# Context rows as 32 tokens at 4 slots, summed in four column groups, with U and V fetched as one row

## What is computed

```
s = jnp.einsum('thpd,hpnd->thpn', qf, sub_keys)
...
act = jax.nn.gelu(jnp.einsum('td,thkd->thk', xb, u_tab[ib]), approximate=False)
return jnp.einsum('thk,thkd->td', gb * act, v_tab[ib])
```

## Time and profile before

| what | value |
|---|---|
| median of three runs | 3763.48 us (3762.64 to 3769.86) |
| the profiled execution's own time | 3768.37 us |
| its span in the trace | 3766.6 us |
| mean granted PE clock | 0.946 |
| busy over the span: PE, DVE, ACT, POOL | 87%, 76%, 25%, 37% |
| data moved over the span | 336 GB/s |

### The profile page before, as it was taken

How to read it: one execution, slowest core, us unless ns; L and a number is a source line. 1 busy time by engine, 2 the same in 40 slices (tenths; PEclk the granted TensorE clock), 3 DMA queues, 4 the chain that set the end, 5 groups by cost and what they waited for, 6 DMA issues and landing times.

```text
span 3766.6 us, 32345 instructions
## 1 busy us (share of the span) xinstructions
PE 3291.4 (87%) x9441; PEld 1672.5 (44%) x9441; DVE 2851.2 (76%) x6490; ACT 928.8 (25%) x2415; POOL 1375.1 (37%) x1205
## 2 busy tenths in 40 slices
PE   7678989987897988577777789999999999999998
PEld 4355434433543444234433444444454444444444
DVE  2637797659767878888898589888787888777776
ACT  1322221355422111146634501011011101110111
POOL 1000554546654445333233222333333333333331
PEclk9889999999998999788998899999999999999999
DMA  9243876768888899999999999999999999999996
GB/s 349 76 176 132 291 247 224 256 221 297 298 307 309 297 346 333 393 360 360 337 396 383 370 365 396 386 404 403 409 411 411 416 391 404 416 409 409 407 409 271
DMA packets 305103, 1269.03 MB, mean 337 GB/s; under 512 B 29456, under 2 KB 79888, under 8 KB 218656
## 3 DMA queue, kind: packets, MB, share of 16 engines
q0 software_dynamic: 169200, 959.16, 65.8%
q1 hardware_dynamic: 134000, 302.17, 21.5%
q10 hardware_dynamic: 1728, 5.64, 0.4%
HBM read 1217.28 MB, written 49.58 MB: 336 GB/s over the span
## 4 chain that ended last, share of the span: by engine, by line
PE 26%; issue 23%; DVE 22%; DMA 19%; POOL 7%; ACT 3%; SPq 0%; DVEq 0%; POOLq 0%; ACTq 0%
DMA arena<-in_uv,idx 7%; DMA ring_e<-in_uv,idx 6%; PE bank L902 5%; PE bank L930 3%; PE wide L845 3%; DMA ring_e<-in_v_rows,idx 3%; PE bank L1064 3%; DVE arena L1873 3%; POOL arena L791 3%; POOL ring_e L791 2%; DVE ring_e L1873 2%; DVE ring_e L1813 2%; PE wide L1114 2%; DVE arena L1904 2%; PE bank L1094 2%
## 5 line engine op out<-in xcount | busy, mean ns | idle before, releaser
L791 POOL DMA_INDIRECT arena<-in_uv,idx x384 | 454.8, 1184 | 845.8 <-PE bank L1126 506.1
L1169 PE MATMUL bank<-arena 128*128 128x384 f32 x2048 | 695.7, 494 | 55.8 <-ACT arena L1569 34.6
L1873 DVE CUSTOM_DVE_ANT_0 arena<-arena,h2e 128x1024 f32<-128x1024 f32 x384 | 460.8, 1220 | 150.3 <-DMA arena<-in_uv,idx 149.3
L1169 PEld LDWEIGHTS bank<-arena 128*128 128x128 f32 x2048 | 392.2, 193 | 370.2 <-issue 136.4
L791 POOL DMA_INDIRECT ring_e<-in_uv,idx x256 | 296.2, 1157 | 618.4 <-PE bank L1126 350.8
L750 POOL DMA_INDIRECT ring_e<-in_u_rows,idx x256 | 330.7, 1292 | 486.7 <-DVE dots_e L1813 332.5
L1182 PE MATMUL wide<-arena 128*128 128x512 f32 x1024 | 462.2, 594 | 5.6 <-DVE arena L1943 5.5
L1512 ACT ACTIVATE small<-small 128x4 f32<-128x4 f32 x160 | 32.7, 205 | 1416.8 <-DVE small L1873 1416.8
L1873 DVE CUSTOM_DVE_ANT_0 ring_e<-ring_e,h2e 128x1024 f32<-128x1024 f32 x256 | 306.8, 1219 | 85.1 <-DMA ring_e<-in_uv,idx 84.9
L1813 DVE CUSTOM_DVE_ANT_0 ring_e<-ring_e,h2e 128x1024 f32<-128x1024 f32 x256 | 303.1, 1219 | 50.6 <-DMA ring_e<-in_u_rows,idx 48.6
L845 PE MATMUL wide<-ring_e,diag_e 128*128 128x512 f32 x520 | 258.7, 638 | 83.4 <-ACT diag_e L1236 55.4
(11 more groups left out here) (265 smaller groups left out, 4424.4 us busy)
## 6 DMA issues: line engine op xcount, KB each, us to landing
arena<-in_ut SPq DMA_DIRECT2D x128, 512.0 KB, 7.9
arena<-in_uv SPq DMA_DIRECT2D x128, 512.0 KB, 8.3
arena<-in_w_q SPq DMA_DIRECT2D x48, 512.0 KB, 6.8
spread_d<-arena SPq DMA_DIRECT2D x12, 2048.0 KB, 25.4
arena<-spread_d SPq DMA_DIRECT2D x96, 256.0 KB, 10.7
ring_e<-in_w_mod POOLq DMA_DIRECT2D x16, 1024.0 KB, 8.1
arena<-in_w_cols SPq DMA_DIRECT2D x24, 512.0 KB, 5.5
arena<-in_x SPq DMA_DIRECT2D x20, 512.0 KB, 4.6
```

The costliest lines, as they stand in the source:

```text
L791: pool.indirect_dma_start(out=ring[r], out_offset=None, in_=a["uv"], in_offset=bass.IndirectOffsetOnAxis(ap=idx[kept(t)][:, k:k + 1], axis ...
L1169: ins = pe.matmul(s_bank[:, 0:NC], lhsT=utb[i % URING][:, k * P:(k + 1) * P], rhs=H2T[1][:, k, P:P + NC], start=(k == 0), stop=(k == KD - 1))
L1873: dve.tensor_tensor_reduce(out=ring[r][:, 0:D], in0=ring[r][:, 0:D], in1=h2b[kept(t)], scale=1.0, scalar=0.0, op0=ALU.mult, op1=ALU.add, a ...
```

## The change

1. **One gather a slot.** U and V come as one 8 KB row of the joint table (`uv`), by one indirect DMA (`gather_row`), which waits for the sum of slot k − 4 (`used_e`). The ring stays at four slots.
2. **Another shape of a slot.** A slot is now 32 tokens at 4 of their experts: partition 32·s + t holds token t's s-th one. `h2e` therefore holds 32 tokens in four copies, in two buffers that change every 32 slots; POOL loads them between the gathers (`load_tokens`, 4 DMAs). `idx` and `gate` of tiles 0 and 1 are put into that order by 16 small DVE operations each in place of one, and `idx_ready` is signalled between the two.
3. **All sums on PE, in column groups.** The weight matrix of a slot is 128x32 (`diag_e[...][:, 0:32]`, made from `sel32`, four 32x32 identities above each other), which adds the four experts of each token. Four matmuls 128x32 by 256 go to the four groups of 32 output partitions, one for each quarter of the row. DVE's sums are gone, and so is `vector_sums`.
4. **The finish of tiles 0 and 1.** Their sums now lie as 32·j partitions by 256·g columns, so the gate, the residual, the squares (`squares_e`, folded over the four quarters by `fold_squares` on PE in beats 1 and 4), the norm and the store run in that layout, with loads and stores in four pieces. SP's load of tile 2's input moves from the start of the last block of score rounds to its round 8.

The core of the diff:

```diff
+        sel32 = gain_reg[:, 3 * P:3 * P + Q]
...
-        hooks, by_vector, at_hook = {}, [], 0
-        for phase, n, vector in (("conv", 16, (False, True)), ("qk", 9, (False,)), ("vg", 16, (False, True)),
-                                 ("ln", 8, (False,)), ("gates", 8, (False,)), ("states", 14, (False,)),
-                                 ("attn", 10, (False,)), ("out", 16, (True,)), ("qf0", 16, (True,)), ("qf1", 16, (True,))):
+        hooks, at_hook = {}, 0
+        for phase, n in (("conv", 16), ("qk", 9), ("vg", 16), ("ln", 8), ("gates", 8), ("states", 14), ("attn", 10),
+                         ("out", 16), ("qf0", 16), ("qf1", 16)):
...
-        def vector_sums(k):
-
-            return k % SLOTS >= EC and by_vector[k // EC]
-
-        def used_e(k):
-
-            return S["used_v" if vector_sums(k) else "used_e"].at(k)
...
-                        sp.wait_ge(*S["dot_e"].at(SLOTS - 1))
-                        load_h2(2)
...
+                        if b == 2 and hp == HP // 2:
+                            sp.wait_ge(*S["dot_e"].at(2 * SLOTS - Q - 1))
+                            load_h2(2)
...
+            def load_tokens(n):
+
+                for i in range(4):
+                    pool.dma_start(h2e[n % 2][i * Q:(i + 1) * Q, :], h2_d[n * Q:(n + 1) * Q, :]
+                                   ).then_inc(*S[f"h2e_in{n % 2}"].mark(n, 16))
+
             pool.wait_ge(*S["h2_out0"].at(0))
-            pool.wait_ge(*S["h2_out1"].at(1))
-            for t in range(2):
-                pool.dma_start(h2e[t], h2_d[t * P:(t + 1) * P, :]).then_inc(*S["h2e_in"].mark(0, 16))
+            for n in range(2):
+                load_tokens(n)
             pool.wait_ge(S["idx_ready"].sem, 1)
 
-            def gather_u(k):
+            def gather_row(k):
 
                 if k == SLOTS:
                     pool.wait_ge(S["idx_ready"].sem, 2)
                 if k >= ERING:
-                    pool.wait_ge(*S["dot_e"].at(k - ERING))
+                    pool.wait_ge(*S["used_e"].at(k - ERING))
                 pool.indirect_dma_start(
-                    out=ring_e[k % ERING][:, 0:D], out_offset=None, in_=a["u_rows"],
+                    out=ring_e[k % ERING], out_offset=None, in_=a["uv"],
                     in_offset=bass.IndirectOffsetOnAxis(ap=idx[k // SLOTS][:, k % SLOTS:k % SLOTS + 1], axis=0)
-                ).then_inc(*landed_u[k % ERING].mark(k, 16))
-
-            def gather_v(k):
-
-                if k >= ERING:
-                    pool.wait_ge(*used_e(k - ERING))
-                pool.indirect_dma_start(
-                    out=ring_e[k % ERING][:, D:2 * D], out_offset=None, in_=a["v_rows"],
-                    in_offset=bass.IndirectOffsetOnAxis(ap=idx[k // SLOTS][:, k % SLOTS:k % SLOTS + 1], axis=0)
-                ).then_inc(*landed_v[k % ERING].mark(k, 16))
-
-            for k in range(2 * SLOTS + V_BEHIND):
-                if k < 2 * SLOTS:
-                    gather_u(k)
-                if k >= V_BEHIND:
-                    gather_v(k - V_BEHIND)
+                ).then_inc(*landed_e[k % ERING].mark(k, 16))
+
+            for k in range(2 * SLOTS):
+                gather_row(k)
+                if k % Q == ERING - 1 and k > Q and k < (2 * SLOTS) - Q:
+                    load_tokens(k // Q + 1)
                 if k == 3:
+                    pool.wait_ge(*S["h2_out1"].at(1))
...
-                    if vector_sums(k):
-                        continue
-                    if k % SLOTS and vector_sums(k - 1):
-                        pe.wait_ge(*used_e(k - 1))
                     pe.wait_ge(*S["diag_e"].at(k))
-                    pe.wait_ge(*landed_v[k % ERING].at(k))
-                    for h in range(2):
-                        ins = pe.matmul(wide[k // SLOTS][:, h * 512:(h + 1) * 512], lhsT=diag_e[k % ERING],
-                                        rhs=ring_e[k % ERING][:, D + h * 512:D + (h + 1) * 512],
-                                        start=(k % SLOTS == 0), stop=(k % SLOTS == SLOTS - 1), skip_group_check=True)
+                    pe.wait_ge(*landed_e[k % ERING].at(k))
+                    c0 = k // Q % 4 * (D // 4)
+                    for j in range(4):
+                        ins = pe.matmul(wide[k // SLOTS][j * Q:(j + 1) * Q, c0:c0 + D // 4], lhsT=diag_e[k % ERING][:, 0:Q],
+                                        rhs=ring_e[k % ERING][:, D + j * (D // 4):D + (j + 1) * (D // 4)],
+                                        start=(k % Q == 0), stop=(k % Q == Q - 1), skip_group_check=True)
                     ins.then_inc(*S["used_e"].mark(k))
...
+            def fold_squares(t):
+
+                pe.wait_ge(*S["y_sum"].at(t))
+                bk = bank(("fold", t))
+                for j in range(4):
+                    ins = pe.matmul(bk[j * Q:(j + 1) * Q, 0:4], lhsT=sel32, rhs=fss[:, 0:4], start=True, stop=True,
+                                    skip_group_check=True)
+                full(ins, ("fold", t))
...
+                if g0 == 0:
+                    act.wait_ge(S["pick"].sem, chain_at(t_ + 1))
...
-                for j in range(0 if vector_sums(k0) else EC):
+                for j in range(EC):
                     act.wait_ge(*S["weight_e"].at(k0 + j))
                     if k0 + j >= ERING:
-                        act.wait_ge(*used_e(k0 + j - ERING))
-                    act.activation(diag_e[r0 + j], ident[:], ACT.Copy, scale=wts_e[:, r0 + j:r0 + j + 1]
+                        act.wait_ge(*S["used_e"].at(k0 + j - ERING))
+                    act.activation(diag_e[r0 + j][:, 0:Q], sel32, ACT.Copy, scale=wts_e[:, r0 + j:r0 + j + 1]
                                    ).then_inc(*S["diag_e"].mark(k0 + j))
...
+            def squares_e(t):
+
+                act.wait_ge(*S["y_pre"].at(t))
+                for g in range(4):
+                    c = slice(g * (D // 4), (g + 1) * (D // 4))
+                    ins = act.activation(ybuf[:, c], x1b[t][:, c], ACT.Square, accum_out=fss[:, g:g + 1])
+                ins.then_inc(*S["y_sum"].mark(t))
...
+                        quarters = [(slice(g * Q, (g + 1) * Q), slice(s * Q, (s + 1) * Q)) for g in range(4) for s in range(4)]
+                        if tile < STREAMS[0][1]:
+                            for g, s in quarters:
+                                done(dve.scalar_tensor_tensor(out=idx[p][s, g], in0=pi[0][g, s], scalar=float(NKEYS),
+                                                              in1=pi[1][g, s], op0=ALU.mult, op1=ALU.add))
+                            after()
+                            dve.sem_inc(S["idx_ready"].sem)
...
+                            hq = PH // 4
+                            for i, (g, s) in enumerate(quarters):
+                                h = slice(i % 4 * hq, (i % 4 + 1) * hq)
+                                done(dve.tensor_tensor(gate[p][s, g].rearrange("p (h k) -> p h k", k=TOPK), g3[g, h, :],
+                                                       gsum[g, h].unsqueeze(2).to_broadcast([Q, hq, TOPK]), ALU.mult))
...
-                    early_sums(c - 1)
                     early_dots(c)
-
-            def early_sums(c):
-
-                for k in range(EC * c, EC * c + EC):
-                    if c < 0 or not vector_sums(k):
-                        continue
-                    t_, r_ = k // SLOTS, k % ERING
-                    dve.wait_ge(*used_e(k - 1))
-                    dve.wait_ge(*S["weight_e"].at(k))
-                    dve.wait_ge(*landed_v[r_].at(k))
-                    dve.scalar_tensor_tensor(out=wide[t_][:], in0=ring_e[r_][:, D:2 * D], scalar=wts_e[:, r_:r_ + 1],
-                                             in1=wide[t_][:], op0=ALU.mult, op1=ALU.add).then_inc(*S["used_v"].mark(k))
...
-                    dve.wait_ge(*S["h2e_in"].at(0))
                 for k in range(EC * c, EC * c + EC):
-                    r_ = k % ERING
-                    dve.wait_ge(*landed_u[r_].at(k))
+                    r_, n = k % ERING, k // Q
+                    if k % Q == 0:
+                        dve.wait_ge(*S[f"h2e_in{n % 2}"].at(n))
+                    dve.wait_ge(*landed_e[r_].at(k))
                     if k >= ERING:
                         dve.wait_ge(*S["gelu_e"].at((k - ERING) // EC))
-                    dve.tensor_tensor_reduce(out=ring_e[r_][:, 0:D], in0=ring_e[r_][:, 0:D], in1=h2e[k // SLOTS], scale=1.0,
+                    dve.tensor_tensor_reduce(out=ring_e[r_][:, 0:D], in0=ring_e[r_][:, 0:D], in1=h2e[n % 2], scale=1.0,
...
+                    dve.wait_ge(*S["mod_rows"].at(2))
+                    dve.tensor_reduce(sel32, ident[:].rearrange("p (s t) -> p t s", t=Q), AX.X, ALU.add
+                                      ).then_inc(*S["sel32"].mark(0))
```

More of the change, by code:

```diff
@@ L311, in build @@
         w_in = [signal(f"w_in{i}") for i in range(WSLOTS)]
-        landed_u = [signal(f"landed_u{i}") for i in range(ERING)]
-        landed_v = [signal(f"landed_v{i}") for i in range(ERING)]
+        landed_e = [signal(f"landed_e{i}") for i in range(ERING)]
```

(20 more changed lines are left out.)

93 lines of the change are left out of this document (65 added, 28 removed).

## The result

The changed kernel takes 4014.04 us (median of 4 runs, 4012.68 to 4017.86) against 3763.66 us (4 runs of the kernel before on the same chip): a ratio of 1.0663 (95% interval 1.0645 to 1.0682), 250 us slower. Its profiled execution has a span of 4015.7 us and a mean granted clock of 0.907, where the one before had 3766.6 and 0.946.

What follows compares the result with a forecast made beforehand. No single engine bounds the kernel: PE paces projections, ln and score rounds, DVE gates and states. Terms 161 + 55 - 43 - 14 + 4 - 2 + 8 + 3 = +172 on 3763.5 give 3935 us, range 3850 to 4030.

Steps and rivals of the forecast that it cites:

- The chain of the score rounds: Score rounds: PE's sums wait for dots behind the copy of scores PE just made, so each round is serial; +161 us.
- PE's idle time in a round: Score rounds, sign in the trace: PE idles some 6 us ahead of the sums, ended by ACT's diagonals; below 2 refutes.
- conv to ln with the start: Projections -43 and ln -14 us from shorter sums on PE; start +3 for tile 0's extra small index operations.
- the ring: Gates and states: a slot is free for the next U row only after its sum; +4 us, between 0 and +37.
- the clock: Score rounds: PE's waits lower the granted clock to 0.81 from 0.97; +55 us, ends 0 and +86.
- attention and all behind the rounds: Attention: smaller diagonals save 0.2 to 0.3 us a hook, -2 us, ends 0 and -24; behind the rounds: 0.
- Rival 4: Ring late everywhere: rows land in 12.3 us, slots freed by the sum; gates and states +37, 3968 us; chance 0.08.
- Out: Output projection: PE gets 17 us of sums, DVE loses 41; +8 us, ends +17 and -24.
- Rival 1: Score rounds: PE doesn't wait, as the diagonals are ready when its scores end; 3710 us; chance 0.06.
- Rival 2: DMA is the limit and 8 KB rows relieve it, 8.6% more rate in the score rounds; 3673 us; chance 0.04.
- Rival 3: Column groups run one after the other, a pair's sums stay at 3.44 us on 89 hooks; 4148 us; chance 0.04.
- Rival 5: It all cancels: waits in the rounds half as long, every gain at its far end; near 3763 us; chance 0.02.

## Why the prediction was right, step by step

**Direction, place and mechanism held.** The loss came out at 250 us where 172 were forecast; 4014 lies within the range, 16 us from its upper end. The chain of the score rounds was put at +161 us at full clock, and the run that keeps PE busy measured +163. PE's idle time in a round was put at some 6 us. It is 5.99 in qf0 (8.45 where a tile is normalised) and 4.03 in qf1, where the chain is shorter, ended by ACT's diagonals each time. The rounds come every 17.3 to 17.6 us in qf0 (19.7 to 20.1 where a tile is normalised) and every 14.7 and 16.0 in turn in qf1 (17 and 15 predicted). Moving the sums by one round took 208 us away, moving the dots by 2 us took 39.

The other 78 us are mostly four terms that missed on the same side: conv to ln with the start 28, the ring 27 (gates and states 13.5, out 13.4), the clock 13.5, and attention and all behind the rounds 6. The range held the time because it left 95 us above the forecast, not because these terms were right.

**The clock was mis-sized by 13 us.** The step took 0.81 on 8.97 us of work, +55; the run measured 68.5. The windows show 0.79 and 0.83, so the mean was right. But PE's work is not spread evenly over it: the sums, which follow the idle time, take 1.94 against 1.07 in all of qf0 but the first round and in every second round of qf1 (1.6 in the others), and the projection behind them takes 8.2 to 9.3 instead of 7.1.

**The ring was priced too low.** The prediction charged gates and states +4 and nothing elsewhere, with a landing of 8 us for two hooks and the clock at its former level outside the rounds. They came out at +17.5, and two gathers bring back 16.6 of it. The single gather also costs 14 us in out and 6 to 8 in conv to ln; attention is 6.5 shorter with it, and the medians differ by 28. Rival 4 named this mechanism and priced it at +37, all in gates and states; the runs put it at half of that there, and at 11 (by the medians) to 16 us (by the traces) elsewhere. A single landing was about right: in gates and states it is 7.6 us in the median, where the half rows of the kernel before took 5.9 and 6.1. But the two gathers of a pair are in flight one behind the other (one pair there was issued at 842.07 and 843.37 and landed at 847.43 and 851.18), and in the median the second lands 9.5 us after the first was issued. And the sums that free the slots take 1.94 instead of 1.05 at a clock of 0.52 in gates. That gives (9.5 + 4.5 + 0.9)/2 = 7.4 a hook, an estimate from these numbers, of the 176.3/22 = 8.0 that were measured; the rest is open. Whether the later release or the longer landing of the 8 KB rows weighs more, no run tells apart, since each changed both.

**Conv to ln gave 26 us of the 57 forecast (54 with the start).** Three things make up most of the gap. The single gather took 8 (446.1 to 438.0). Tile 1's rearranging was left out: the prediction counted tile 0's 15 extra small operations before its first gather, and not that tile 1's 32 run in the midst of the q/k projections, ahead of DVE's convolution step and of the dots that PE waits for. The timeline of DVE and PE in the changed kernel:

```profile
513.24 3.40 DVE L1794 SCALAR_TENSOR_TENSOR idx<-pi 32x32 uint32<-32x32 f32 x16
...
517.35 3.40 DVE L1815 TENSOR_TENSOR gate<-ge,small 32x32 f32<-32x32 f32 x16
520.78 2.98 DVE L2070 TENSOR_SCALAR arena<-arena,cw,cvv 128x1024 f32<-128x1024 f32 x4
...
524.86 1.22 DVE L1849 CUSTOM_DVE_ANT_0 ring_e<-ring_e,h2e 128x1024 f32<-128x1024 f32 x1
...
528.24 1.93 PE L836 MATMUL wide<-ring_e,diag_e 128*32 128x256 f32 x16 [7.01 <-ACT diag_e L1241]
```

The two rows of 16 take 6.8 us, where two single operations took 0.29 each before, and PE waits 7 us for the dots behind them. In the kernel with the new layout for tile 0 only, the sum at the same place waits 0.89:

```profile
517.38 1.07 PE L863 MATMUL wide<-ring_e,diag_e 128*32 128x256 f32 x16 [0.89 <-ACT diag_e L1271]
```

There conv to ln were another 6.8 shorter than with two gathers alone (438.0 to 431.2). And a pair costs 1.19 on the path, not 1.05: hooks of v come every 8.06 us, less 6.87 for the projection. Over the 49 hooks that is 7. What is left of the gap, some 6 us, was not tried; kernels with the same code in these stages differ by 5.

**Out:** +8 was right for the sums alone (152.1 with two gathers, +7.1); the rest of the +21.4 goes with the gather.

**Rivals 1, 2, 3 and 5** are out: PE waits 4 to 6 us a round; the single gather by itself makes the kernel before 30 us slower, with DMA as busy in the rounds as it was; a pair takes 1.07 of PE's time, so the column groups run at once; and nothing cancelled.

## What to carry to other kernels

Before work is moved to another engine, look at what stands directly ahead of it there and at what its inputs wait for: a piece that needs an answer to the instruction just before it turns two engines that ran side by side into a chain, whatever the piece itself costs. The cure is to take the piece one round late and put it where the longest independent work covers the answer's way; here that gave back 208 of 231 us. And a change that pays in one stage and hurts in another can often be split by data, here by tile, so that each stage keeps the form that suits it.

## What the runs showed of the hardware that was not expected

Adding 150 matmuls whose result nobody reads made the kernel 68 us faster: with PE busy in its waits the granted clock was 0.99 and 0.97 (2.4 GHz nearly throughout) instead of 0.79 and 0.83, and a pair's sums took 1.07 us instead of 1.94.

Column groups among full matmuls cost more on the path than the context stream's rows let expect. There two changes of shape cost 0.14 us; here the hook's 8.06 less 6.87 leaves 1.19, of which 0.86 is the work of four groups at once by the prediction's estimate, and 0.33 is left for two changes and the second slot's wait, which no run tells apart. The score rounds agree: without a sum they came every 7.76 us before, with a sum and no wait every 8.95, 1.19 more. The Trainium skill, "TensorEngine Tiling (Array Packing)", Tiling Modes, says that changing the mode drains TensorE. The measured 1.19 stands nearer to the 1.28 that the prediction worked out for such a drain than to the 1.05 that it took; the difference of 0.14 makes some 12 us over the 89 hooks.

Two gathers of 4 KB rows with a wait each beat one gather of 8 KB rows in both layouts, by 30 and by 28 us, though POOL issues 256 gathers fewer with the single one. Two things differ: with two gathers the U half of a slot is free as soon as its dot is made, and each half lands sooner (5.9 and 6.1 us in the median of gates and states before, against 7.6). How much each is worth was not tried.
